# An even slot order, later ScalarE steps and half-size weight splits in the expert stage of a two-layer hybrid model kernel

## What is computed

```python
def swiglu(h, w1, w3, w2):
    return (jax.nn.silu(h @ w1) * (h @ w3)) @ w2

def moe_swiglu(h, w_router, w1, w3, w2):
    logits = (xt @ w_router).astype(jnp.float32)
    top_logits, top_idx = lax.top_k(logits, TOP_K)
    gates = jax.nn.softmax(top_logits, axis=-1)
    ...
    def expert_block(args):
        x_blk, e = args
        return swiglu(x_blk, w1[e], w3[e], w2[e])
    yb = lax.map(expert_block, (xb, block_expert)).reshape(p_len, d)
    y = jax.ops.segment_sum(yb * gate_buf[:, None].astype(yb.dtype), tok_buf, num_segments=n)
```

## Time and profile before

| | |
|---|---|
| median of 3 executions | 1795.31 us (1790.07 to 1795.5) |
| the profiled execution | 1791.45 us, its span 1789.8 us |
| PE busy | 1671.0 us, 93% of the span |
| DVE busy | 1396.6 us, 78% |
| ACT busy | 1017.1 us, 57% |
| DMA, mean over the span | 281 GB/s |
| TensorE's granted clock | 0.977 of 2.4 GHz |

### The profile page before, as it was taken

One profiled execution on the slowest core, in us unless ns is written; L12 is line 12 of the kernel. 1 busy time (PEld: TensorE's weight loads), 2 busy tenths in 40 slices (PEclk: granted clock), 3 DMA queues, 4 the chain that ended last, 5 costly groups with the idle time before them and its releaser, 6 DMA issues.

```text
span 1789.8 us, 23460 instructions
## 1 busy us (share of the span) xinstructions
PE 1671.0 (93%) x8869; PEld 1372.4 (77%) x8869; DVE 1396.6 (78%) x1438; ACT 1017.1 (57%) x967; POOL 57.6 (3%) x84
## 2 busy tenths in 40 slices
PE   5999979999999899999999999999999999999996
PEld 5988868999898877778776766776677766788875
DVE  4887677888787775897687878877877887888877
ACT  1644533343453443766667667676766676667663
POOL 1000100000100001000000000000000000010120
PEclk9998999999998898999999999999999999999999
DMA  9545656888544563997899889889998999999993
GB/s 309 163 152 166 233 167 224 270 285 277 191 151 158 180 218 135 371 344 275 322 341 338 325 317 355 326 327 339 353 331 310 340 352 344 333 380 358 362 388 147
DMA packets 270304, 503.70 MB, mean 281 GB/s; under 512 B 12646, under 2 KB 113272, under 8 KB 270200
## 3 DMA queue, kind: packets, MB, share of 16 engines
q1 hardware_dynamic: 262736, 489.72, 77.5%
q0 software_dynamic: 3072, 11.01, 1.7%
q10 hardware_dynamic: 4392, 1.57, 0.4%
HBM read 492.84 MB, written 9.44 MB: 281 GB/s over the span
## 4 chain that ended last, share of the span: by engine, by line
issue 43%; PE 36%; DVE 12%; ACT 4%; POOL 1%; DMA 1%; ACTq 1%; DVEq 1%; POOLq 1%; SPq 0%
PE ps L1898 7%; PE ps L1900 7%; PE ps L1899 7%; DVE lo_ring L1806 7%; PE ps L2227 4%; PE ps L2226 4%; ACT stage_hi L1169 3%; PE ps L2355 3%; DVE lo_ring L1550 2%; DMA weight_ring<-in_moe_w_dram 1%; PE ps L2190 1%; ACT stage_hi L1099 1%; DVE xn L1841 1%; POOL rstd L828 1%; POOL y_back L892 0%
## 5 line engine op out<-in xcount | busy, mean ns | idle before, releaser
L1806 DVE TENSOR_TENSOR lo_ring<-weight_ring,stage_hi 128x2048 fp32r<-128x2048 f32 x210 | 473.8, 2288 | 124.0 <-ACT stage_hi L1169 123.3
L1169 ACT CAST stage_hi<-weight_ring 128x2048 fp32r<-128x2048 f32 x210 | 395.0, 1911 | 22.0 <-DMA weight_ring<-in_moe_w_dram 21.3
L1550 DVE TENSOR_TENSOR lo_ring<-weight_ring,stage_hi 128x2048 fp32r<-128x2048 f32 x126 | 283.7, 2287 | 40.9 <-ACT stage_hi L1099 40.2
L1099 ACT CAST stage_hi<-weight_ring 128x2048 fp32r<-128x2048 f32 x126 | 235.3, 1912 | 45.2 <-DMA weight_ring<-in_moe_w_dram 44.3
L1898 PE MATMUL ps<-h_hi,stage_hi 128*128 128x256 f32 x800 | 233.2, 291 | 8.9 <-DVE h_lo L1263 7.1
L1300 DVE TENSOR_TENSOR lo_ring<-weight_ring,stage_hi 128x2048 fp32r<-128x2048 f32 x81 | 184.9, 2292 | 69.0 <-ACT stage_hi L964 61.6
L1899 PE MATMUL ps<-h_lo,stage_hi 128*128 128x256 f32 x800 | 229.3, 287 | 0.0
L1900 PE MATMUL ps<-h_hi,lo_ring 128*128 128x256 f32 x800 | 229.0, 286 | 0.0
L964 ACT CAST stage_hi<-weight_ring 128x2048 fp32r<-128x2048 f32 x81 | 153.6, 1905 | 125.8 <-DMA weight_ring<-in_w_in_dram 63.5
L1898 PE MATMUL ps<-stage_hi,xe_hi 128*128 128x512 f32 x448 | 182.3, 407 | 8.3 <-DVE lo_ring L1550 6.9
L1899 PE MATMUL ps<-lo_ring,xe_hi 128*128 128x512 f32 x448 | 177.2, 396 | 0.0
(11 more groups left out here) (379 smaller groups left out, 2613.8 us busy)
## 6 DMA issues: line engine op xcount, KB each, us to landing
weight_ring<-in_moe_w_dram SPq DMA_DIRECT2D x336, 1024.0 KB, 7.3
weight_ring<-in_w_mod_dram SPq DMA_DIRECT2D x48, 1024.0 KB, 5.5
weight_ring<-in_w_in_dram SPq DMA_DIRECT2D x36, 1024.0 KB, 5.4
weight_ring<-in_ffn_w_dram SPq DMA_DIRECT2D x33, 1024.0 KB, 7.7
weight_ring<-in_w_out_dram SPq DMA_DIRECT2D x12, 1024.0 KB, 4.9
moe_rows<-y_moe POOLq DMA_DIRECT2D x6, 512.0 KB, 5.2
moe_rows<-y_e POOLq DMA_DIRECT2D x3, 512.0 KB, 8.5
x_tok<-in_x_dram SPq DMA_DIRECT2D x1, 1024.0 KB, 10.8
```

Source lines behind the costliest of these rows:

```text
L1099: nc.scalar.copy(jst_hi[i % JSTAGES][:], ring[:, n % RING, :]).then_inc(hi_ready, 1)
L1169: nc.scalar.copy(jst_hi[g % JSTAGES][:], ring[:, n % RING, :]).then_inc(hi_ready, 1)
L1550: nc.vector.tensor_tensor(ring_lo[:, n % RING, :], ring[:, n % RING, :], raw(jst_hi[i % JSTAGES][:]), ALU.subtract).then_inc(lo_ready, 1)
L1806: nc.vector.tensor_tensor(ring_lo[:, n % RING, :], ring[:, n % RING, :], raw(jst_hi[g % JSTAGES][:]), ALU.subtract).then_inc(lo_ready, 1)
```

## The change

It has three parts.

**The order and the tables.** The small slots behind the six B slots go from 3, 3, 6, 6, 3, 3 to 4, 4, 3, 5, 4, 4 (in the first chunk the second number is smaller by two); the last chunk keeps its 6, 6, 6, 6, 2, 0. ACT's steps `s1`, `s3`, `silu`, `rows`, `hi` and `bsilu` stand behind a later slot. DVE's `act` and `lo` keep their place, `bsum` goes one later. `bT` goes one slot earlier, and `bhi` and `blo` with it. PE's `places(1)` moves to directly ahead of its use.

**The banks.** `sT` writes SGATE in place of SUP, `rows` writes SUP. What waits for `s_ac` is then the small experts' w3 slot, and no longer the w1 slot two places before it.

**The halves.** ACT's and DVE's splits of all 336 expert slots are each made by two instructions of 1024 columns, each with its own signal, and PE waits for the first half ahead of its first matmuls with it and for the second half ahead of the ones that need it. The split of the 81 slots ahead of the experts is as before, and so are the DMAs (1 MB each) and PE's work.

```diff
-        behind = [3, 1 if ch == 0 else 3, 6, 6, 3, 3] if ch < NCH - 1 else [6, 6, 6, 6, 2, 0]
+        behind = [4, 2 if ch == 0 else 4, 3, 5, 4, 4] if ch < NCH - 1 else [6, 6, 6, 6, 2, 0]
...
 def b_at(ch):
-    return AT["B", "w3", ch, 1] + 3
+    return AT["B", "w3", ch, 1] + 2
...
-                     *[(AT["S", "w1", c, 1] + 2, ("s1", c)) for c in CS], *[(AT["S", "w3", c, 1] + 2, ("s3", c)) for c in CS],
...
+                     *[(AT["S", "w3", c, 0] + 2, ("s1", c)) for c in CS], *[(AT["S", "w3", c, 1] + 2 + (c < LAST_C), ("s3", c)) for c in CS],
...
+        def parts_of(i, job=0):
+
+            here = 0 if isinstance(job, int) else job * (2 * JOB_SLOTS) + 2 * G_SLOTS
+            return [here + (ND + 2 * i + part + 1) for part in range(2)]
...
-                nc.scalar.copy(jst_hi[g % JSTAGES][:], ring[:, n % RING, :]).then_inc(hi_ready, 1)
+                for part in map(columns, range(2)):
+                    nc.scalar.copy(jst_hi[g % JSTAGES][:, part], ring[:, n % RING, part]).then_inc(hi_ready, 1)
...
-                        nc.scalar.activation(s_silu, ps[:, SUP, 0:FCH // 2], ACT.Silu).then_inc(s_sl, 1)
+                        nc.scalar.activation(s_silu, ps[:, SGATE, 0:FCH // 2], ACT.Silu).then_inc(s_sl, 1)
...
-                dve.wait_ge(hi_ready, GD + g + 1)
-                nc.vector.tensor_tensor(ring_lo[:, n % RING, :], ring[:, n % RING, :], raw(jst_hi[g % JSTAGES][:]),
-                                        ALU.subtract).then_inc(lo_ready, 1)
+                for part, count in zip(map(columns, range(2)), parts_of(JOB_SLOTS + g)):
+                    dve.wait_ge(hi_ready, count)
+                    nc.vector.tensor_tensor(ring_lo[:, n % RING, part], ring[:, n % RING, part],
+                                            raw(jst_hi[g % JSTAGES][:, part]), ALU.subtract).then_inc(lo_ready, 1)
...
                     if kind == "w1" and h == 0:
+                        if c and c % NCH == 0:
+                            pe.wait_ge(gx_lo, 5 + c // NCH)
+                    if kind == "w3" and h == 0:
                         if c:
                             pe.wait_ge(s_ac, c)
```

More of the change, by code:

```diff
@@ L1548, in split_of @@
                 n = NS + i
[L1549 to L1551 removed]
+                for part, count in zip(map(columns, range(2)), parts_of(i, job)):
+                    dve.wait_ge(hi_ready, count)
+                    nc.vector.tensor_tensor(ring_lo[:, n % RING, part], ring[:, n % RING, part],
+                                            raw(jst_hi[i % JSTAGES][:, part]), ALU.subtract).then_inc(lo_ready, 1)
             def select(table, column, places=posj):
@@ L2354, in _ @@
                                 at = b * (FCH // 2) + k * SMALL
-                                last = mm(ps[:, SUP, at:at + SMALL], part[:, k * P:(k + 1) * P], fold[:], start=True, stop=True)
+                                last = mm(ps[:, SGATE, at:at + SMALL], part[:, k * P:(k + 1) * P], fold[:], start=True, stop=True)
                         last.then_inc(s_tp, 1)
                     elif step == "rows":
-                        gather_small(c)
+                        gather_small(c, SUP)
                     elif step == "bT":
```

73 lines of the change are left out of this document (40 added, 33 removed).

## The result

The changed kernel takes 1778.54 us (median of 7 executions, 1776.21 to 1783.49); the kernel before, measured beside it, 1791.19 us (7 executions, 1789.53 to 1799.82). The ratio is 0.9929, with a 95% interval of 0.9905 to 0.9953. The gain is some 12.7 us, where 35 to 39 were forecast: the sign is right, the size isn't, and the time lies above the forecast range of 1745 to 1774. The profiled execution of after took 1780.87 us, its span 1779.2.

The account below looks back on a forecast made before the run. PE, busy 93% of the span, was taken to set the time, so only its stops counted. Gains of 32.8 (group), 4.0 (first expert) and 3.9 (loop), 40.7 less 3.7, gave 37: 1754.5, plus 1.5, 1756 us; range 1745 to 1774.

Parts of the forecast that it names:

- The ceiling: PE's stops in first expert, group and loop: removing all would gain at most 51.0 us, a floor of 1740.5 us.
- the opening stop: PE's stop for ACT's `s3` at the group's start: 1.6 + 0.26 us, expected to stay, 1.9 us.
- Rival 4: Whole kernel: stops only move from one wait to another, time stays at 1788 to 1798 us; chance 0.05.
- rival 3: ACT's and DVE's new order locks, PE's w3 waits: 2.3 us for each of 28 c, about 1815 us; chance 0.08.
- the same instructions elsewhere: zero: Moved steps `places`, `rows`, `bT`: no cost, up to 2 us either way for the range.
- the even order: Group: removes runs of six S slots in six of seven chunks, costs nothing: same slots, same matmuls.
- The slack arithmetic: Ring of six buffers: slack 1.9 us with whole splits, 3.8 with halves; six S slots need 3.1.
- First expert: First expert's stage: all but 0.5 us of its 4.5 us of PE stops goes, gain 4.0 us.
- The hand-over: Stop of 2.85 us at the loop's start: only half a split, 1.07 us, is saved.
- the loop: Loop behind the hand-over: the 1.75 us stop goes with its 0.26, half the short ones stay; gain 2.0 + 0.8 us.
- The halves' prices: Two halves against one whole split: +0.07 us on DVE, +0.1 on ACT, hidden under PE.
- rivals 1 and 2: Supply limits: ring of six buffers, about 1771 us, chance 0.14; single transfers' own rate, 1768 or so, chance 0.03.

Follow-up runs that it names:

- e1: The kernel before with the split halves alone, its order, tables and banks kept: 1746.19 us, ratio 0.9750.
- e3: The changed kernel with ACT's `s1` and `s3` of c = 0 alone one and two slots earlier: 1770.9 us, ratio 0.9873.
- e4: The changed kernel with DVE's `act` and `lo`, and also `bhi` and `blo`, one slot later: 1761.96 us, ratio 0.9831.
- e11: The changed kernel with only `bhi` and `blo` one slot later: 1770.6 us, ratio 0.9880.
- e6: The changed kernel with the edits of e3 and e4 together, ACT's `rows` one slot earlier and its `sum` one later: 1748.41 us, ratio 0.9772.
- e8: Like e6 (halves, new banks, ACT's late steps with all the mending), but in the old slot order: 1749.15 us, ratio 0.9774.
- e2: The changed kernel with whole splits of 2048 columns, so new order, tables and banks alone: 1806.05 us, ratio 1.0070.
- e12: e1 with splits in four parts of 512 columns, each with its own wait on PE: 1750.7 us, ratio 0.9763.

## Why the prediction was wrong, and where it was right

**The ceiling was right.** "All three together: 51.0 us" was the most that PE's standing could return. e1 returned 46.2.

**The forecast's size was right for the wrong kernel.** The prediction's group of 634 us, its supply of 350 GB/s, and a time of 1756 are met, or beaten, by e1 (633.3 us, 353 GB/s, 1746.2 us), which has the halves and nothing else. The sum kept 7 of 39.8 us of stops in the group; the group kept all of them in another form, 668.95 us for 667.80. The step that failed is the pricing of the moved steps and of the order, which came before the sum: "They now allow ACT to be three slots ahead of PE ... The 152 us of ACT's waits mostly go; what is late next is the data." The waits did go. But a step of ACT is also something that others wait for, and the two sides have to be worked out together:

- At the opening I kept "1.9 for the opening stop (1.6 + 0.26)". It is 5.18 us of idle time, and 7.6 us in all by e3. The ring isn't full there: slots still come at the pace of the transfers (ACT waited 2.82 and 0.90 us for them), so that `s3`, three slots behind the slot it copies and no longer two, is not there when PE comes, a B slot earlier than before. Rival 4 named the mechanism ("`s3` now stands one slot later, and PE's `sT` waits for it") but gave it no place of its own.
- "DVE's `act` and `lo` keep their places, while ACT's silu and `hi` ... come one slot later" was rival 3, with 0.08. It was at work: DVE's 26 waits of 43.0 us for the silu, and 16.6 us by e4. But not as written: PE nowhere waited at w3 for `act`. DVE stood at `lo`, and PE stopped a slot later for the split that was queued behind it. That the price of 2.3 us per c is near the stop of 2.05 is therefore luck in part. And it hit 6 of 28 c, those without a B slot between `sT` and the next w3. I had counted them ("in 21 of 27 cases a B slot of 5.6 too") and then said of the other six that the chain "fits, by 1.7 us, if ACT has finished its split by then". It hadn't: `bhi` had held it for 2.02 us. The condition stood in the text and wasn't priced.
- `bT` one slot earlier was among "the same instructions elsewhere: zero", and `bhi` and `blo`, which go with it, were not costed at all. `bhi` stands two slots behind `bT` in both kernels, and before ACT waited there 0.7 us in all. Once its other steps no longer hold it, ACT comes to `bhi` ahead of PE and waits 13.9 us: a hold taken away at one step shows up at the next. By e11 one slot more is worth 8 us.
- "I cost it at nothing", of the even order: it is worth nothing in itself (e6 against e8), but the places of the other steps had been written for the old one. There exactly one B slot stands between each `sT` and the next w1 slot. In the new one the opening's `sT` comes ahead of a B slot that it followed before, six c have no B slot up to the next w3, and `rows` has none: the stops of 1.40 us there are in every run with the new order and in none with the old.

Together the terms that I set to zero or near it were worth 32 us (e1 to after). How they share it is known for the opening (7.6) and for the pair at `lo` and `bhi` (16.6), and open for the rest. Without the halves they exceed what the late steps give, and e2 comes out slower than before.

**The gains of two remedies were for the same stops.** The prediction gave each remedy a paragraph, and one sum for both, and did not ask what either would do alone. The slack arithmetic had the answer: 1.9 us with whole splits, short by 1.2 for six S slots, 3.8 with halves, so that the halves alone cover all six. The sentence that the last chunk's sixes fit "if ACT is not held" was too strict: in e1 ACT is held for 103.5 us, and of its stops in the group those for DVE are small, 0.38 to 1.11; the opening keeps 1.69.

**Right by the step:**
- First expert: 4.0 forecast, 4.1 seen.
- The hand-over: "only half a split, 1.07 us, is saved". 2.85 less 1.07 is 1.78, and 1.78 us is what stands at 1517.09.
- The halves' prices, +0.07 us on DVE and +0.1 on ACT for a pair: 2.36 to 2.29 and 2.00 to 1.91. No fresh half cost DVE more than 1.22 us.
- PE's extra waits at zero: the loop, with twice the waits, runs 243.94 us busy of 245.
- Supply: 353 GB/s over e1's whole group; rivals 1 and 2 fall.

**Missed on the other side: the loop**, by 3.7 us (6.5 for 2.8). The prediction took the clock as full there. In before's windows of 10 us it is 0.83 at 1520 and at 1720, behind the two longest stops, and matmuls start 0.43 us apart for about 3.4 us after each: 8 starts or so of 0.2 us too much, 1.6 us per stop. With the stop of 1.75 gone and the other down to 1.78, neither fall is there in after, and the windows read 1.00. That accounts for 3.2 of the 3.7.

The Trainium skill (Perfetto Trace Analysis, section Optimizing Scalar/DVE Operations) says that where ScalarE or VectorE aren't saturated but leave bubbles on other engines, smaller instructions may let work finish sooner. The trace agrees: DVE is busy 78% of the span before and ACT 57%, and e1 gains 2.5%. The runs also show a limit: quarters gain nothing more.

## What to carry to other kernels

A step that one engine takes out of its queue for another has two constraints, and moving it later relaxes one and tightens the other. For every step moved, write down the last slot whose data it now waits for and the first instruction elsewhere that waits for it, at the beginning of the stage and at each place where the usual cover is missing, and move its partners on the other engines along. When a change holds two remedies, work out each alone first: if both cure the same stops, the sum is the larger one, and the second brings only its risks. Here the smaller change, halves alone, is as fast as any kernel that ran, 1746.2 us; e6, e8 and e12 can't be told from it.
